# First attention of a two-block kernel: key splits, gate scans and output gates in another place

## The reference, cut to what matters

```python
xn = rmsnorm(x, norm_g) * (1 + scale_x) + shift_x
aq, ak, av, az, mq, mk, mv, mo, mz, mi, mf = project(xn, w_in)
q = rope_2d(aq, tables); k = rope_2d(ak, tables)
att_x = window_ctx_attention(q, k, v, kc, vc, sink) * jax.nn.silu(az)
xq, xk = mlstm_qk(mq, mk, conv_w, conv_b)      # silu(dwconv(...))
h_lat, _ = mlstm_bidir(xq, xk, mv, mi + b_i, mf + b_f, ctx_state)
m_x = mlstm_post(h_lat, mo, mz, head_g)
x = x + gate_x * (concat([att_x, m_x]) @ w_out)
```

## Time and profile before

| | us |
|---|---|
| median of 3 runs | 2941.73 (2938.67 to 2943.05) |
| the profiled execution | 2941.7 |
| its span in the trace | 2939.9 |
| PE busy | 2742.1 (93%) |
| DVE busy | 1566.7 (53%) |
| ACT busy | 984.9 (34%) |
| POOL busy | 301.0 (10%) |

### The profile page before, as it was taken

The page is one execution under the profiler, slowest core; times in us unless marked ns, Lnnn a source line. Parts: engine busy times, 40 slices in busy tenths (PEclk is TensorE's granted clock), DMA queues, the critical chain, the costliest instruction groups (busy, mean ns, idle before and its releaser), DMA issues. The chain is left out here.

```text
span 2939.9 us, 38758 instructions
## 1 busy us (share of the span) xinstructions
PE 2742.1 (93%) x15704; PEld 2269.4 (77%) x15704; DVE 1566.7 (53%) x2476; ACT 984.9 (34%) x1829; POOL 301.0 (10%) x260
## 2 busy tenths in 40 slices
PE   6999998999897899898989879998899999999998
PEld 3788887879765798786869758865688888888887
DVE  4302556778642612656758544868844444444445
ACT  3201232555521411323546324358722112112112
POOL 0000001221431000002213410000100000000001
PEclk7999998999998899998999989999999999999999
DMA  6322322006454313321034440100300101101102
GB/s 267 98 84 75 85 75 73 12 15 212 144 221 165 111 60 83 92 81 44 16 126 148 142 158 30 46 22 1 116 35 29 58 29 57 57 29 57 57 33 88
DMA packets 111559, 244.89 MB, mean 83 GB/s; under 512 B 10962, under 2 KB 66180, under 8 KB 103088
## 3 DMA queue, kind: packets, MB, share of 16 engines
q1 hardware_dynamic: 90256, 228.03, 22.8%
q10 hardware_dynamic: 21152, 14.75, 1.6%
HBM read 194.51 MB, written 42.99 MB: 81 GB/s over the span
## 5 line engine op out<-in xcount | busy, mean ns | idle before, releaser
L923 PE MATMUL ps<-xn_hi_sb,ft_hi_sb 128*128 128x512 f32 x720 | 263.2, 366 | 7.4 <-DVE ft_lo_sb L1346 7.4
L924 PE MATMUL ps<-xn_lo_sb,ft_hi_sb 128*128 128x512 f32 x720 | 262.9, 365 | 0.0
L925 PE MATMUL ps<-xn_hi_sb,ft_lo_sb 128*128 128x512 f32 x720 | 262.5, 365 | 0.0
L2946 DVE TENSOR_TENSOR arena_sb<-arena_sb,ps 128x512 f32<-128x512 f32 x256 | 173.0, 686 | 121.4 <-PE ps L2625 118.8
L871 PE MATMUL ps<-tm_hi_sb,xn_hi_sb 128*128 128x512 f32 (+2 forms) x608 | 215.3, 354 | 0.8 <-DVE xn_lo_sb L1273 0.8
L873 PE MATMUL ps<-tm_hi_sb,xn_lo_sb 128*128 128x512 f32 (+2 forms) x608 | 212.8, 350 | 0.0
L872 PE MATMUL ps<-tm_lo_sb,xn_hi_sb 128*128 128x512 f32 (+2 forms) x608 | 212.3, 349 | 0.0
L2584 PE MATMUL ps<-xn_hi_sb,w_up_hi_sb 128*128 128x512 f32 x512 | 199.3, 389 | 0.0
L2586 PE MATMUL ps<-xn_hi_sb,w_up_lo_sb 128*128 128x512 f32 x512 | 199.2, 389 | 0.0
L2585 PE MATMUL ps<-xn_lo_sb,w_up_hi_sb 128*128 128x512 f32 x512 | 199.2, 389 | 0.0
L2623 PE MATMUL ps<-w_down_hi_sb,h_hi_sb 128*128 128x512 f32 x480 | 186.7, 389 | 0.0
(11 more groups left out here) (412 smaller groups left out, 6167.3 us busy)
## 6 DMA issues: line engine op xcount, KB each, us to landing
arena_sb<-in_w_ft SPq DMA_DIRECT2D x44, 512.0 KB, 3.6
arena_sb<-mqk_dram SPq DMA_DIRECT2D x36, 512.0 KB, 3.4
arena_sb<-x_dram SPq DMA_DIRECT2D x33, 512.0 KB, 6.5
arena_sb<-in_w_ada SPq DMA_DIRECT2D x16, 1024.0 KB, 8.4
arena_sb<-in_w_up SPq DMA_DIRECT2D x16, 1024.0 KB, 6.6
arena_sb<-in_w_down SPq DMA_DIRECT2D x16, 1024.0 KB, 4.8
arena_sb<-in_xall SPq DMA_DIRECT2D x20, 512.0 KB, 4.6
arena_sb<-mv_dram SPq DMA_DIRECT2D x40, 256.0 KB, 3.8
```

The costliest lines, as they stand in the source:

```text
L923: pe.matmul(to, hi, xn_hi_flat[:, k, at:at + size], start=k == 0, stop=False)
L924: pe.matmul(to, hi, xn_lo_flat[:, k, at:at + size], start=False, stop=False)
L925: mm = pe.matmul(to, lo, xn_hi_flat[:, k, at:at + size], start=False, stop=k == KT - 1)
```

## The change

- The attention gate's fourth tile becomes the last projection tile (17); mq and mk move up by one (9 to 16). The host's order of weights follows.
- ACT's rounding of the keys and DVE's key splits (now all four remainders on DVE) move into the rope part of `ft`, after the second and third rope. POOL's first query split runs when the ropes are done; its second when all tiles are done. Rounded keys, first queries and the window mask get other places in SBUF, and SP loads the mask at the start of `ft`.
- `gate_scans` is cut: `low_ft` for tile 9 goes between the two sums, for tile 10 before the last maximum; `gate_rests` and `gate_decays` follow convolutions 0, 1 and 2. ACT's four exponentials follow the eviction of tile 12; PE's transposes and decays stand before tiles 15 and 16, in banks 6 and 7; DVE evicts them after convolutions 5 and 6.
- The spreads of the output gates move into `output`: PE after turn(1) and, in the first layer, again after turn(2), both into banks 6 and 7; ACT copies them, before gate(2) and after it.

The core of the diff:

```diff
-N_GATE, N_K, N_Q, N_AZ, N_MQ, N_MK = 0, 1, 2, 6, 10, 14
+N_GATE, N_K, N_Q, N_AZ, N_MQ, N_MK, N_END = 0, 1, 2, 6, 9, 13, 17
...
 # PE, ft
                     for n in range(N_AZ + 1, F_TILES):
-                        tile(n, nt * P if n < N_MK else NTOK)
-
-                    pe.wait_ge(g_exp[l], 4)
-                    pe.wait_ge(ft_ev[l], F_TILES)
...
+                        if n == N_MK + 2:
+                            pe.wait_ge(g_exp[l], 4)
+                            turn_rows(row_a, 6)
+                            turn_rows(row_w, 7)
+                            for i in range(2 * MH):
+                                mm = pe.matmul(ps[:, 6, 400 + NTILE * i:400 + NTILE * (i + 1)], sel[:, i, :], m_dec[:, :], start=True, stop=True)
+                            mm.then_inc(g_tr[l], 1)
+                        if n == N_MK + 3:
+                            pe.wait_ge(g_cols[l], 2)
+                            turn_rows(row_b, 7)
+                        tile(n, NTOK if N_MK <= n < N_END else nt * P)
 # PE, attention
-                    pe.wait_ge(g_cols[l], 4)
-                    pe.wait_ge(ft_rope[l], 5)
                     pe.wait_ge(a_mask[l], 16)
+                    pe.wait_ge(ft_ev[l], F_TILES - 1)
...
                     scores(0, 0, 0, 0, WIN)
+                    pe.wait_ge(ft_ev[l], F_TILES)
                     scores(1, 0, 0, 1, WIN)
-                    pe.wait_ge(gt_ev, 1)
+                    pe.wait_ge(g_cols[l], 4)
 # PE, output
                     turn(1, 1)
+                    spread_gate(l, 0)
                     second_half(0, 0)
                     second_half(1, 1)
                     turn(2, 0)
+                    if l < DEPTH - 1:
+                        spread_gate(l, 1)
+                        pe.wait_ge(gt_ev, 2)
                     modulation(0)
 # DVE, ft
+                        if r in (1, 2):
+                            split_keys(l, r - 1)
...
-                    low_ft(N_MQ)
...
-                        dve.wait_ge(ft_az_st[l][u], 32)
+                        dve.wait_ge(ft_az_st[l][u], 32 - 16 * u)
...
                         if N_MQ + c + 2 < F_TILES:
                             low_ft(N_MQ + c + 2)
+                        if c < 2:
+                            gate_rests(l, c)
+                        if c == 2:
+                            gate_decays(l)
+                        if c == 5:
+                            gate_columns(l, 0)
+                            gate_columns(l, 1)
...
+                        if c == 6:
+                            gate_columns(l, 2)
 # ACT, ft
+                        if r == 1:
+                            high_keys()
...
+                        if c == 3:
+                            gate_exponentials()
                         silu(c, c % 2, ntok)
+                    attention_gate(3, N_END, N_END % 2)
 # ACT, output
                     gains(1, 1)
+                    spread_gate(0)
                     gate(2, 0)
+                    if l < DEPTH - 1:
+                        spread_gate(1)
                     for t in range(nt):
                         if t + 3 < nt:
                             gate(t + 3, (t + 3) % 2)
 # POOL, attention
                     pool.wait_ge(ft_rope[l], 5)
-                    pool.wait_ge(ft_mm[l], F_TILES)
                     split_queries(0)
+                    pool.wait_ge(ft_mm[l], F_TILES)
...
-                    pool.tensor_tensor(k_lo[own, at], k_raw[own, at], k_hi[own, at].bitcast(F32), ALU.subtract).then_inc(a_k[l], 1)
                     split_queries(1)
```

More of the change, by code:

```diff
@@ L194, in host_layout @@
         q, z = [[np.concatenate([m[:, DH * j:DH * (j + 1)], m[:, DH * (j + 4):DH * (j + 5)]], 1) for j in range(4)] for m in (aq, az)]
-        w_ft.append(np.stack([rows(m) for m in [ak] + q + z + sum([np.split(m, 4, 1) for m in (mq, mk)], [])]))
+        w_ft.append(np.stack([rows(m) for m in [ak] + q + z[0:3] + sum([np.split(m, 4, 1) for m in (mq, mk)], []) + z[3:]]))
     for b, kept in enumerate(w_tm):
@@ L371, in build @@
         h_z = [part(CST + 384 + 512 * u, MW) for u in range(2)]
-        gate, gate_c, final_g = part(ACC, D_MODEL), part(ACC + 1024, D_MODEL), part(ACC + 1024, D_MODEL)
+        gate_x, gate_c, final_g = part(ACC, D_MODEL), part(ACC + 1024, D_MODEL), part(ACC + 1024, D_MODEL)
         sq_junk = part(CST + 1408, MW)
@@ new lines, in rows, with split_keys @@
+                def rows(g):
+                    return slice(g * DH, (g + 1) * DH)
+                def split_keys(l, g):
+                    own, other, at = rows(g), rows(1 - g), slice(P + g * NTOK, P + (g + 1) * NTOK)
+                    dve.tensor_copy(k_hi[other, at], k_raw[own, at])
+                    dve.wait_ge(a_kh[l], g + 1)
+                    dve.tensor_tensor(k_lo[other, at], k_raw[own, at], k_hi[own, at].bitcast(F32), ALU.subtract).then_inc(a_kl[l], 1)
+                    dve.wait_ge(a_kl[l], g + 1)
+                    dve.tensor_tensor(k_lo[own, at], k_raw[own, at], k_hi[own, at].bitcast(F32), ALU.subtract).then_inc(a_k[l], 1)
@@ L1443, in ft @@
                                  [(q_flat[:, r - 1, SEQ:NTOK], everything)] if nt > NX else None)
+                        if r == 1:
+                            for k in (k_hi, k_lo):
+                                dve.tensor_scalar(k[:, 0:P], ident[:, :], 0.0, None, ALU.mult)
+                        if r in (1, 2):
+                            split_keys(l, r - 1)
                     dve.wait_ge(ft_rope[l], 5)
@@ L1692, in output @@
                             columns_of(ada_after, l + 1, 7)
-                        residual(t, t % 2, gate if t < NX else gate_c)
+                        residual(t, t % 2, gate_x if t < NX else gate_c)
                         if t + 2 < nt:
@@ L1816, in raw, with high_keys @@
                         act.activation(cst[u][:, 0:ntok], ps_flat[:, 1536 * u:1536 * u + ntok], ACT.Copy).then_inc(ft_ev[l], 1)
+                    def high_keys():
+                        act.wait_ge(ft_rope[l], 1)
+                        for g in range(KV):
+                            own, at = slice(g * DH, (g + 1) * DH), slice(P + g * NTOK, P + (g + 1) * NTOK)
+                            act.activation(k_hi[own, at], k_raw[own, at], ACT.Copy).then_inc(a_kh[l], 1)
                     for r in range(5):
@@ L1895, in query_block @@
                                 act.activation(sink_e[:, u, :], sink_e[:, u, :], ACT.Exp).then_inc(a_sink_e[l], 1)
-                    act.wait_ge(ft_silu[l], 8)
-                    for g in range(KV):
-                        own, at = slice(g * DH, (g + 1) * DH), slice(P + g * NTOK, P + (g + 1) * NTOK)
-                        act.activation(k_hi[own, at], k_raw[own, at], ACT.Copy).then_inc(a_kh[l], 1)
                     exps(0, 0, 0, WIN)
```

124 lines of the change are left out of this document (48 added, 76 removed).

## The result

The changed kernel takes 2911.82 us (median of 4 runs, 2910.52 to 2915.71) where the kernel before takes 2940.2 (median of 4, 2938.64 to 2943.05): ratio 0.9905, 95% interval 0.9887 to 0.9922, 28.4 us less. The forecast was 2914.3, range 2903 to 2926. The profiled execution took 2912.02 us (span 2910.3), its mean granted clock 0.971.

The account below looks back on a forecast made before the run. PE, busy 93% of the span, was taken as the bound, with holes at boundaries and ft_lo waits. Terms -39.0 + 8.0 + 2.4 - 1.2 - 10.6 + 0.7 + 3.3 + 9.0 = -27.4 from 2941.7 gave 2914.3 us, range 2903 to 2926.

Parts of the forecast that it names:

- The boundary: Last projection tile's end (T) to first transposes, each layer: T + 4.1 instead of 23.6 us, -39.0 in all.
- Table loads: ACT at the boundary: number of loads unchanged, one of 1.28 us on the path; the skill's 1.38 us drain left out.
- The stream: Transposes and decays moved between projection tiles: 4.0 us per layer, +8.0; a possible clock fall 1.2 per layer, +2.4.
- Gate scans: Second layer's projections: both waits for ft_lo and the slow clock after them go, -10.6.
- the term for POOL: Projections: POOL's first query split slows DVE's first gate rows, two operations at 0.5 us each, most paid: +0.7.
- Attention at full clock: Attention's first heads ran at half clock and may not any more: -0.6 per layer, -1.2.
- Output, first layer: First spread costs little; ACT waits for the second ahead of gate(3), so product(2) starts later: +9, ends 5 and 12.
- Output, second layer: One spread before second_half(0); ACT's copy delays gate(2) and the chain to product(2): +3.3, ends 1.7 and 4.5.
- the stall at ft_lo: Rival, second layer's projections: low_ft held again, 10.6 lost and up to 5 more, 2925 to 2930; chance 0.13.
- the output wait: Rival, output: gate(3) not held, the 9 and half of the 3.3 vanish, about 2904; chance 0.09.
- wait for residual(t - 1): Rival, first layer's output: look-ahead lost, each of seven products pays +6.1, 43 in all, 2957; chance 0.04.
- rival 4: Holes only move: clock falls in both layers' streams, tile 17's eviction or the splits wait; gain under 6 us; chance 0.05.

Follow-up runs that it names:

- experiment 1: Kernel after, with ACT's copy of the second output spread issued behind gate(3) instead of ahead of it, first layer: 2909.88 us (before: 2935.6 on this chip).
- those six: Profiles of the kernel after and five variants of it with the same projections: 12 stretches, the clock fell in 7 and not in 5.
- experiment 9: Kernel after, with the tile order of before (a key convolution last, attention gates as tiles 6 to 9): 2937.45 us (before: 2938.83).
- experiment 11: Kernel after once more, unchanged, on another chip: 2915.8 us, ratio 0.9923 to the kernel before.
- experiment 4: Kernel after, with the splitting of the keys put back to the start of attention on ACT and DVE: 2933.64 us (before: 2935.6).
- experiment 3: Kernel before, with only two of DVE's low_ft (tiles 9 and 10) moved among the gate scans: 2928.07 us (before: 2935.6).
- Experiment 5: Kernel after, with the first output spread between turn(0) and turn(1), the second between the second halves, its copy behind gate(3): 2900.59 us (before: 2938.61).
- experiment 10: Kernel after, with output spreads in PE's waits, gate rows and decays in attention's first heads, POOL's first query split after tile 13: 2895.58 us, ratio 0.9853 to before.

## Why the prediction was right, point by point

**The boundary**: forecast T + 4.1, found T + 4.02 and 3.80; -39.4 for -39.0. The reason given ("none of it but scores and transposes needs the last tile") stands, yet it counted work, not price. PE's transposes, decays and spreads lay beside DVE's queue and cost PE's path nothing; what held it was the convolution with its eviction (10.2 us), DVE's copies (1.7), the keys on DVE and POOL (10.1) and the scores behind them (1.7). The forecast took PE's moves out of the hole as if they had filled it; its sum was right because it was made from the new chain, not from what was removed.

**Table loads**: at the new boundary the load runs from 491.50 to 492.78 and the exponential starts at 492.80. By the Trainium skill's 1.38 us of drain (ScalarE: Activation LUTs, What ACT_TABLE_LOAD costs) the boundary would be 5.4 us; the trace has 4.02, so the row was the better guide.

**The stream**: 4.0 forecast for the transposes and decays, 4.2 found (238.73 or 238.75 less 234.50). The clock was put at 1.2 us per layer; it is 0 or 1.6. The rows of the kernel after behind its light work, and the same place of experiment 1, where the clock did not fall:

```profile
442.50:446.00 3.50, 3.50 (x39) 3.40 (x38) 1.99 (x2) 1.30 (x2) 0.00 (x0) 1.00 0.49 150
446.90:450.40 3.50, 3.50 (x10) 2.78 (x9) 3.43 (x3) 0.58 (x1) 0.00 (x0) 0.53 0.00 0
```

```profile
446.70:453.00 6.30, 6.30 (x28) 5.18 (x29) 6.19 (x5) 1.94 (x2) 0.00 (x0) 1.00 0.00 0
```

Eight profiles hold the light work in one piece (those six and experiments 9 and 11), in 16 stretches: the clock fell to its lower level (1.2 GHz) in 9 and not in 7, each fall at 1.6 us. So 1.2 was fair as a mean and false as a value.

**Gate scans**: -10.6 forecast, -10.9 when moved alone. In the kernel after 0.99 us of it is lost to a wait one tile earlier, at tile 8. That is the term for POOL, put at 0.7 with ends 0 and 1.5; "most of it paid" was right, but the two operations lose 0.43 and 0.97 us, not 0.5 each. So a tile does wait for ft_lo, which the prediction had named as a sign of being wrong: its term for POOL leads to low_ft for tile 8, but it did not carry that wait over into its list of signs. The wait is no work of the key splits: with the keys back in attention (experiment 4) the wait was 1.02 us.

**Attention at full clock**: -0.6 per layer was forecast, -1.3 and -2.1 found for attention and mLSTM together. Most of that is the mLSTM, 0.9 and 1.7 us shorter, which no edit touches; attention itself is 0.5 and 0.4 shorter. The mechanism shows: before, half clock lasts 3.6 and 3.7 us beyond the first transposes, in the kernel after the granted clock is 1.00 there. The size is not shown: in experiment 11 the clock fell for 3.4 us in the first layer's boundary and attention, and attention was 0.2 us longer and 1.6 shorter than before.

**Output, first layer**: the mechanism came out as written: ACT waits on the spread ahead of gate(3), and product(2) starts late, by 10.1 us for the 9 forecast. The 1 us is lost ahead of gate(3), which starts 36.8 us behind the stage's first matmul where the text had 35.8; from there to product(2) it is 9.0 us, written as 8.9. The wait at the next layer's weights gave 1.8 back, which the text had excluded ("nothing is got back"); the net is 8.2. Against experiment 3, with the same output code as before, it gave 0.7 back, so this is no firm number. What the text lacked is that only half is ACT's order. The first spread, "the first spread costs little", takes 3.78 us at half clock. The half clock behind it is no extra cost: it lasts some 10 us there in one piece, but before it came twice, for 3.4 and 3.5 us, and in experiment 3, with no spread in the output, once for 6.9, and the count in experiment 1 comes out without it.

**Output, second layer**: +3.3 forecast, +2.8 found in this profile and +3.6 to +3.8 in the eight others with the same code, so 3.3 was fair. Experiment 5 takes all of it away.

Of the rivals none came whole: the stall at ft_lo shrank to 1.0 us, the output wait was not hidden, and product(t) did not come to wait for residual(t - 1). Of rival 4 the clock came, in both layers of this profile, but neither the eviction nor the splits hold anything.

**The total**: the trace gives 29.6 us for the 27.4 forecast. The 2.2 us between them are what attention and mLSTM gave beyond their term, most of it in the mLSTM, which nothing touches. The other errors cancel: the second layer's projections won 1.3 us less than forecast, the output stages lost 1.3 less. So the mechanisms were right, and that the total is within some 2 us is luck.

## What to carry to other kernels

Price a hole by the chain that ends it, engine by engine, and not by what the waiting engine does in it: five and a half us of PE work in this hole cost nothing but the 1.7 us of copies that it left to DVE, and moved into a full stream it cost 4.2, or 5.9 with the clock. Put light work where its engine waits anyway, and put it early in that wait, before the clock has fallen. When an instruction that waits is set into an in-order queue, write down what stands behind it: one copy ahead of gate(3) cost 5.4 us, and two instructions moved among the scans gave 10.9.

## What the runs showed of the hardware

- Whether the granted clock falls behind the same 3.3 us of light matmuls differs between executions of one kernel (in both layers of one profile, in neither of the next); over all it fell in 9 of 16 stretches. The decays alone, 1.9 us, had it fall once in two. The first spread of the output, issued behind a wait of PE of 2.83 us, took 3.78 us for four passes in eight of nine profiles (3.20 in experiment 11); issued in that wait it took 1.98 us (first layer, experiments 5 and 10), and the turn behind the wait was at half clock all the same (1.11 us, experiment 5).
- Beside POOL's split, DVE's operations on two inputs slow down by 0.9 to 1.1 us each: 1.49 to 2.46 us, 1.23 to 2.14, and the first of the keys' subtractions 1.48 to 2.36 and 2.58 in experiment 4.
- Stretches that no kernel here touches differ between profiles by 2 to 3 us in one piece (the first layer's mLSTM 103.9 or 106.6; from the last output matmul of the second layer to PE's last 1199.7 to 1200.4 in ten profiles and 1202.6 to 1203.0 in three), more than most single edits are worth.
